# Strassen panels of a hybrid decoder layer: third product ahead of the sixth, S1's product between sixth and seventh, S3 and S1 split ahead of the up block

## The reference

```python
def swiglu(x, w_gate, w_up, w_down):
    return (jax.nn.silu(x @ w_gate) * (x @ w_up)) @ w_down

x = x + 0.5 * swiglu(rmsnorm(x, ffn1_norm), ffn1_w_gate, ffn1_w_up, ffn1_w_down)
# ... input projection, mLSTM branch, differential attention, output projection ...
x = x + 0.5 * swiglu(rmsnorm(x, ffn2_norm), ffn2_w_gate, ffn2_w_up, ffn2_w_down)
```

## Time and profile before

| | us |
|---|---|
| median of 3 runs | 1613.79 |
| lowest, highest | 1613.22, 1616.24 |
| the profiled execution | 1615.87 |
| its span in the profile | 1614.1 |

### The profile page before, as it was taken

How to read it: one execution, slowest core, us unless ns; L and a number is a source line. 1 busy time by engine, 2 the same in 40 slices (tenths; PEclk the granted TensorE clock), 3 DMA queues, 4 the chain that set the end, 5 groups by cost and what they waited for, 6 DMA issues and landing times.

```text
span 1614.1 us, 29927 instructions
## 1 busy us (share of the span) xinstructions
PE 1570.3 (97%) x12266; PEld 1488.0 (92%) x12266; DVE 1019.3 (63%) x1675; ACT 687.2 (43%) x1125; POOL 4.5 (0%) x20
## 2 busy tenths in 40 slices
PE   8899999999999999999999999999998999999998
PEld 8899999999988678999999966779998999999997
DVE  5988888433682455733346689674458888886333
ACT  5555455222332445521211258572246555555222
POOL 0000000000000000000000000000000000000000
PEclk9999999999999999999999999999999999999999
DMA  6233333322352661233433250553322333323321
GB/s 151 79 105 101 83 105 84 104 76 79 90 179 57 207 197 48 78 92 91 149 99 96 70 193 27 199 168 91 91 78 79 105 105 105 105 79 109 90 79 67
DMA packets 247117, 169.22 MB, mean 105 GB/s; under 512 B 8382, under 2 KB 229811, under 8 KB 246746
## 3 DMA queue, kind: packets, MB, share of 16 engines
q1 hardware_dynamic: 246712, 167.04, 35.6%
q10 hardware_dynamic: 290, 0.57, 0.1%
HBM read 147.73 MB, written 18.71 MB: 103 GB/s over the span
## 4 chain that ended last, share of the span: by engine, by line
PE 85%; DVE 6%; ACT 4%; issue 2%; DMA 2%; SPq 0%; DVEq 0%; ACTq 0%
PE ps L469 41%; PE ps L1011 25%; PE ps L967 3%; PE ps L1360 2%; PE ps L1324 1%; PE ps L1511 1%; PE ps L1409 1%; PE ps L1154 1%; PE ps L1203 1%; PE ps L1636 1%; PE ps L1566 1%; DVE small L3192 1%; PE ps L1680 1%; DMA xtok<-in_x_sample 1%; ACT w_hi L436 1%
## 5 line engine op out<-in xcount | busy, mean ns | idle before, releaser
L436 ACT ACTIVATE w_hi<-raw 128x1024 fp32r<-128x1024 f32 (+1 forms) x110 | 126.6, 1152 | 411.8 <-PE ps L469 395.5
L469 PE MATMUL ps<-xn_hi,w_hi 128*128 128x272 f32 (+1 forms) x848 | 245.7, 290 | 0.7 <-issue 0.7
L469 PE MATMUL ps<-xn_hi,w_lo 128*128 128x272 f32 (+1 forms) x848 | 246.1, 290 | 0.0
L469 PE MATMUL ps<-xn_lo,w_hi 128*128 128x272 f32 (+1 forms) x848 | 245.1, 289 | 0.0
L440 DVE TENSOR_TENSOR w_lo<-raw,w_hi 128x1024 fp32r<-128x1024 f32 (+1 forms) x110 | 147.3, 1340 | 154.9 <-ACT w_hi L436 154.7
L469 PE MATMUL ps<-h_hi,w_hi 128*128 128x280 f32 (+1 forms) x572 | 166.1, 290 | 0.0
L469 PE MATMUL ps<-h_hi,w_lo 128*128 128x280 f32 (+1 forms) x572 | 165.8, 290 | 0.0
L469 PE MATMUL ps<-h_lo,w_hi 128*128 128x280 f32 (+1 forms) x572 | 165.2, 289 | 0.0
L469 PEld LDWEIGHTS ps<-xn_hi,w_hi 128*128 128x128 f32 x848 | 159.8, 188 | 1.5 <-issue 1.3
L469 PEld LDWEIGHTS ps<-xn_hi,w_lo 128*128 128x128 f32 x848 | 159.7, 188 | 0.0
L469 PEld LDWEIGHTS ps<-xn_lo,w_hi 128*128 128x128 f32 x848 | 159.3, 188 | 0.0
(11 more groups left out here) (517 smaller groups left out, 3870.1 us busy)
## 6 DMA issues: line engine op xcount, KB each, us to landing
raw<-in_w_in SPq DMA_DIRECT2D x55, 512.0 KB, 3.9
rawg<-in_ffn_w_gate SPq DMA_DIRECT2D x44, 512.0 KB, 4.1
rawu<-in_ffn_w_up SPq DMA_DIRECT2D x44, 512.0 KB, 5.3
raw<-in_ffn_w_down SPq DMA_DIRECT2D x32, 704.0 KB, 4.6
pages<-in_cache_k SPq DMA_DIRECT2D x16, 512.0 KB, 4.3
pages<-in_cache_v SPq DMA_DIRECT2D x16, 512.0 KB, 4.6
Cb<-in_state_C SPq DMA_DIRECT2D x24, 256.0 KB, 4.1
out<-Cb SPq DMA_DIRECT2D x24, 256.0 KB, 2.2
```

The costliest lines, as they stand in the source:

```text
L436: act.activation(w_hi[s][:, 0:p.nk, :], raw[s][:, 0:p.nk, :], ACT.Copy).then_inc(hi_done[s], 1)
L469: mm = pe.matmul(ps[:, bank + half, 0:p.half], w[s][:, k, :], x[:, i, cols], start=first and k == 0 and a == 0, stop=last and k == p.nk - ...
```

## The change

Three orders are changed, and no instruction is added or removed. On TensorE, p3 of panel j-1 moves from sixth to fourth place in a pass, and the product with S1 from fourth to sixth; p6 stays fifth and p7 seventh. On ScalarE, `u_split` moves from behind `s2_split` to behind `s31_split`, which stands behind `third_sum`. On VectorE, `s31_rest` and `u_rest` change places behind `up_sum`. The two tables follow.

```diff
@@ PRODUCT7
-                            + [x for j in panels7 for x in (("p1", j), ("p2", j), ("p4", j - 1), ("p6", j),
-                                                            ("p3", j - 1), ("p7", j))]
+                            + [x for j in panels7 for x in (("p1", j), ("p2", j), ("p4", j - 1), ("p3", j - 1),
+                                                            ("p6", j), ("p7", j))]
@@ SPLIT7
-                          + [(n, j) for j in panels7 for n in ("g", "s2", "u", "s31")])
+                          + [(n, j) for j in panels7 for n in ("g", "s2", "s31", "u")])
@@ TensorE, strassen
                     fourth(p, turn, j - 1)
+                    third(p, turn, j - 1)
+                    sixth(p, turn, j)
                     after(pe, lo7, SPLIT7, turn, "s31", j)
                     if j >= F + 2:
                         after(pe, gate7, GATE7, turn, "g2", j - 2)
                     seventh(p, s1, 3, c + 1, first=True)
-                    sixth(p, turn, j)
-                    third(p, turn, j - 1)
                     seventh_last(p, turn, j)
@@ ScalarE, panels_of (the same move ahead of it, for the panel behind F, in both turns)
                         s2_split(turn, j + 1)
-                        u_split(turn, j + 1)
                     gate(p, turn, j - 1, "g2")
                     third_sum(p, turn, j)
                     if j + 1 < FT:
                         s31_split(turn, j + 1)
+                        u_split(turn, j + 1)
@@ VectorE, panels_of
                     up_sum(p, turn, j - 1)
+                    s31_rest(turn, j)
                     u_rest(turn, j)
-                    s31_rest(turn, j)
```

More of the change, by code:

```diff
@@ L2175, in _ @@
             s2_split(0, 3)
-            u_split(0, 3)
             third_sum(up1, 0, 2)
             s31_split(0, 3)
+            u_split(0, 3)
             first_sum(up1, 0, 3)
@@ L2456, in _ @@
             s2_split(1, 1)
-            u_split(1, 1)
             third_sum(up2, 1, 0)
             s31_split(1, 1)
+            u_split(1, 1)
             first_sum(up2, 1, 1)
```

## The result

The changed kernel takes **1615.7 us** (median of 22 runs, 1614.6 to 1618.2) where the kernel before takes 1614.0 in the same sessions (22 runs, 1612.8 to 1616.2). The ratio is 1.0012, with a 95% interval of 1.0006 to 1.0017. So the change costs about 1.7 us. The interval lies wholly above 1, so the loss is real; it is inside the 0.2% called no change and the time is inside the range, but the forecast was 1614.1, or +0.3.

The account below looks back on a forecast made before the run. TensorE was taken to bound the kernel, with the VectorE-ScalarE loop close behind. Terms -1.2 - 0.2 - 1.0 + 1.9 + 0.8 = +0.3 us gave a median of 1614.1 us, range 1611.3 to 1616.0.

Parts of the forecast that it names:

- ring of 10.6: VectorE and ScalarE feeding each other: period per panel grows from 10.02 by 0.60 to 10.62 us, slower than TensorE's 10.51.
- Turn 0, forecast -1.2: Turn 0: wait for S31's low tile in panel 3 and a small p4 delay go, saving 1.2 us.
- the 10.85 that I named as a sign: Turn 0: up_sum starts 10.85 us apart, TensorE's own pace there, if the forecast is right.
- Turn 1, panels 1 and 2, forecast -0.2: Start of turn 1: waits worth 1.6 us go, but p7 then waits longer for p6's read; 0.2 us remains saved.
- Turn 1, panels 2 to 21, forecast -1.0 + 1.9: Turn 1: 1.0 us saved from panel 2 to 3, then 18 panels lose 0.11 us each, +1.9 us.
- p1 within 0.1 us of G's low part all through the turn: Turn 1: sign that VectorE paces TensorE; p1 starting 1 us or more behind would mean 2 to 3 us lower.
- Last panel, forecast +0.8: Turn 1's last panel: hidden-tile copies end late against p6 because VectorE's lead is gone, costing 0.8 us, 1.2 at most.
- Down projection and loads of SyncE, forecast 0: After the last p7: down projection follows as before, and the rawg and rawu loads are unaffected, 0 us.
- The cited rule on VectorE: VectorE operations each waiting for an empty pipe: period 11.8 us, turn 1 over 20 us slower; given no chance.
- That the ring doesn't bind: Rival, turn 1: period stays at 10.51 us or less, turn 1 keeps its gain, -2.5 us, 1611.3 us; chance 0.22.
- Late loads in turn 1's panels: Rival: late loads, no longer absorbed by VectorE's idle time, go straight to the end; 1618.9 us; chance 0.09.
- That the norm's sequence gives way by itself: Rival, turn 1's panel 1: p6's read isn't held by table loads; -3.9 us, 1609.9 us; chance 0.04.

Follow-up runs that it names:

- the wait filled: Changed kernel with VectorE's hidden_2 moved between up_sum and S31's low part, into the wait for S31's copy; 1612.46 us, 0.9991 of the kernel before.
- the old last panel: Changed kernel, but in the last panel U is split ahead of S31 on ScalarE and VectorE, as before; 1614.35 us, 1.0000 of the kernel before.
- the rewritten norm pass: TensorE's new order, old splits; in turn 1's panel 1, p6's read and G's split precede Silu's table load, G's low part and hidden_1 precede S1; 1611.90 us.
- p6 fourth: Kernel before with TensorE's order p1, p2, p4, p6, S1's product, p3, p7, splits as before; 1614.08 us, 0.9994 of the kernel before.

## Why the prediction was right, and where it was off

The mechanism was right: no wait on S31's low tile, 0.60 us lost in each round, a ring of 10.6 that TensorE has to follow in turn 1, and a new wait in the last panel. That the measured time lies inside the range is in part luck. The range was added up from the bounds of its own terms, and nearly the whole of the miss is a term that isn't among them. Those bounds also sum to +1.8, which is 1615.6 on the base of 1613.8 that the sum uses and not the 1616.0 stated; the measured +1.7 just fits.

**Turn 0, forecast -1.2, measured -0.95.** The wait went, and p1 of panel 4 starts at 71.35 in place of 72.58, 1.23 earlier, with G's low part done at 71.30: the room was as worked out. What came on top is TensorE's own pace, 10.866 a panel in the new order in place of 10.853, about 0.2 us over 17 panels. The sum had no term for it. The ring is 10.66 here, not the 10.85 that I named as a sign: VectorE stays on its own period for some ten rounds, until it has its lead back, and only then follows TensorE.

**Turn 1, panels 1 and 2, forecast -0.2.** Measured 13.47 in place of 13.61 from p1 of panel 1 to p1 of panel 2, -0.14. The wait for the read of p6 is 2.65, as the 2.5 said. That 1.4 of 1.6 us stay in the norm's sequence is right. In the second profile of the changed kernel this stretch is 13.91, since the clock fell earlier; in the two kernels below that keep both new orders here and show no fall it is 13.42 and 13.43, which is the -0.2.

**Turn 1, panels 2 to 21, forecast -1.0 + 1.9, measured +0.44.** From p1 of panel 2 (1247.11) to that of panel 21 (1448.39) it is 201.28 in place of 200.84. Both ends stand right behind G's low part, so this is 19 rounds of a ring of 10.594; the mechanism was right and the size of a round was 0.026 too large. The added 0.60 is exact. The 10.02 to which I added it was one round with an idle column of 0.82; others have 0.78 and make 9.99 to 10.02. Nineteen rounds make 0.5 us of 0.026; a period should be a mean over several rounds, not one.

In one respect the picture differs. I had p1 within 0.1 us of G's low part all through the turn. In the profile TensorE lost about 1.5 us in panel 2 to the clock (11.99 from p1 to p1, where 10.53 is usual for it without the fall), so VectorE had a lead of that size, and TensorE ran at its own 10.45 until the ring, 0.14 longer a round, had used the lead up: the first p1 that lasts 0.39 again is that at 1363.64. The end is the same, since both ends of the stretch hang on the ring.

The same rows show the price better than my comparison did. TensorE's own pace in the new order is 10.45, not 10.51. So the ring costs 0.14 a panel against what this order could have given, and the forecast's 0.11 against the old pace (measured, 10.594 - 10.51 = 0.08) was a comparison with the kernel before only.

**Last panel, forecast +0.8, measured +0.77.** A wait for `sq` of 0.46 where 0.6 was said, and the copies of the hidden tile at 1456.01, 7.62 after p1 of the panel in place of 4.89. Its reason, the lead that VectorE has lost, is borne out by the kernel with the wait filled, in which it is gone. It is gone with the old last panel too, so it takes the last round's 0.60 us besides.

**Down projection and loads of SyncE, forecast 0, measured +1.48.** This is the step that failed, and it holds nearly all of the miss (+0.3 forecast, +1.65 measured). I followed the loads `rawg` and `rawu`, and wrote that the down projection "follows p7 as before". But SyncE's queue also waits for U's low part of the last panel ahead of the down weights, and that is the one event that the new split order delays by construction, by 1.73 us. The lost lead delays it by another 2.13 (forecast: 2.1). Before, the load was 1.56 us ahead of its need, and with the first delay alone (the wait filled) no wait shows; of both together, 1.5 us came through. An event whose place changes has to be followed to everyone who waits for it, and U's low part has three listeners: TensorE's p4, the loads of `rawu`, and this one.

**The cited rule on VectorE.** The prediction takes from the Trainium skill ("VectorE: DVE Perf Modes", section "The DRAIN you can't avoid") that an operation waits for an empty pipe, and finds that the rows disagree. The same paragraph of that section adds that an operation which isn't held starts earlier. Starts 0.08 us ahead of the end before them, as at 1263.87 and at 1442.65 above, agree with that, so the rows don't contradict the page.

**The rivals.** That the ring doesn't bind fell: VectorE's 0.60 is whole in each round, and taking 0.35 of it back frees TensorE at once. Late loads in turn 1's panels were not seen in the changed kernel's two profiles; the slow load was another. That the norm's sequence gives way by itself fell too, and when it is made to, most of the gain is lost again a panel later.

**The sum again, from measured terms:** -0.95 - 0.14 + 0.44 + 0.77 + 1.48 = +1.6, and the medians say +1.7. Of the two halves of the change, TensorE's is worth -2.2 to -2.7 us (its two medians against before), and on top of it the split order costs 4.3 (1616.80 against 1612.47 in one session). TensorE's half, with or without the rewritten norm pass (1611.90 to 1612.47), is faster than the kernel before and the changed one; filling the wait on top of it was not tried.

## What to carry to other kernels

When two engines feed each other, add up the loop's own period, from one start of a piece to the next, and compare it with the period of the engine that sets the end: 0.6 us of new idle time on an engine that is 63% busy cost more than the wait it was to cure. Of an operation that moves later, list everyone who waits for its semaphore, queues of loads for the *next* stage included; the last pass of a loop is where they stand. And where two edits cure the same wait, run each alone: here one of them held the whole gain, and on top of it the other only cost.

## What the runs showed of the hardware

**The clock fell in some executions only.** After the 2.45 to 2.70 us wait in panel 1 TensorE's granted clock fell in three of eight profiles that have this wait (both of the changed kernel, one of the two of TensorE's order alone), to 0.51 from 1247.0 to 1250.4 in the clearest one. That is the 1.2 GHz level: 15 matmuls stand 0.227 apart, where 0.125 is usual (10.51 us for 84). It cost 1.5 us when TensorE set the pace, and nothing when the ring did. The kernel before waits 1.25 there, with shorter waits ahead, and shows no fall. Nor is this the only place: five of the other profiles (the kernel before, the old last panel, the wait filled, the rewritten norm pass, p6 fourth) have one stretch of 20 us with a clock of 0.91 between 1000 and 1080 us, in code that no edit touches, and the first profile of TensorE's order alone and that of the split order have none at all. The Trainium skill ("TensorE: Matmul & The Clock Gate", section "What's actually happening") says that the chip's look at TensorE's activity isn't aligned with the start of the kernel. That one kernel shows the fall in one profile and not in the other agrees with it; no run here tests it further.

**A run's time goes with its mean clock.** The record has the mean granted clock of every execution, from 0.992 to 0.998. In the second session's 33 runs of the kernel before, the six at 0.998 have a median of 1614.0, the 23 at 0.997 or 0.996 one of 1614.8, and the four at 0.995 or less one of 1618.2. A straight line through the 33 gives 0.9 us for each 0.001, and through the runs of the four kernels of that session 0.9 to 1.1. That is as much as the differences between several kernels here. It doesn't explain what the change costs: the changed kernel's second set of runs has a mean clock of 0.9961, TensorE's order alone 0.9962 and the kernel before 0.9964, so that the 4.3 and 2.2 us between the first and the other two stand. A run's mean doesn't say where the clock fell, so the share of panel 2 in it stays open.

**TensorE's own pace depends on the order of the products.** With the same 84 matmuls a panel, a full clock and no wait in sight, a panel of turn 1 takes 10.51 us in the order before, 10.45 in the new one and 10.53 with p6 fourth; in turn 0 it is 10.853, 10.866 and 10.833. The order that is best in turn 1 is worst in turn 0. Over 18 panels that is up to 1.4 us, which is as much as the waits in question. I have no cause for it, and the runs don't settle one.
